# Row-tiled scores and a softplus split into a high and a low half, in the stick-breaking attention of a two-layer hybrid decoder step

## The reference, cut to what matters

```python
z = jnp.einsum('bqhd,bkhd->bhqk', qb, kb).astype(jnp.float32) * scale + bf
log_stop = jnp.where(mask, jax.nn.log_sigmoid(-z), 0.0)
after = lax.cumsum(log_stop, axis=3, reverse=True) - log_stop
A = jnp.where(mask, jnp.exp(jax.nn.log_sigmoid(z) + after), 0.0)
outs.append(jnp.einsum('bhqk,bkhd->bqhd', A.astype(v.dtype), vb))
```

## Time and profile before

| | |
|---|---|
| median of 3 runs | 1691.22 us (1683.71 to 1696.84) |
| span of the profiled execution | 1684.9 us |
| instructions in it | 22304 |
| mean granted TensorE clock | 0.956 |
| sweeps of the second layer, pair 0, 1, 2 | about 912 to 1055, 1135 to 1282, 1346 to 1525 us |

### The profile page before, as it was taken

The page is one execution under the profiler, slowest core; times in us unless marked ns, Lnnn a source line. Parts: engine busy times, 40 slices in busy tenths (PEclk is TensorE's granted clock), DMA queues, the critical chain, the costliest instruction groups (busy, mean ns, idle before and its releaser), DMA issues. The chain is left out here.

```text
span 1684.9 us, 22304 instructions
## 1 busy us (share of the span) xinstructions
PE 1550.3 (92%) x8356; PEld 1254.9 (74%) x8356; DVE 751.6 (45%) x1181; ACT 691.0 (41%) x1339; POOL 578.9 (34%) x471
## 2 busy tenths in 40 slices
PE   5899998999999999999759999989989999989995
PEld 3877698766797666899548767977658976669994
DVE  4332317976353334341661323278763533333417
ACT  5344512444524545443343344224444245445423
POOL 2353412535223333142443433115441242431325
PEclk8999979999999999999879999899999999999998
DMA  6400023100221000241252000230002200003213
GB/s 237 155 26 26 13 60 82 51 26 1 73 75 51 26 13 14 67 139 51 96 170 90 25 26 13 90 84 32 13 13 85 70 32 26 14 27 113 92 42 125
DMA packets 75672, 103.69 MB, mean 62 GB/s; under 512 B 14370, under 2 KB 61218, under 8 KB 75426
## 3 DMA queue, kind: packets, MB, share of 16 engines
q1 hardware_dynamic: 64176, 60.64, 11.1%
q10 hardware_dynamic: 11378, 41.53, 7.7%
HBM read 74.26 MB, written 27.88 MB: 61 GB/s over the span
## 5 line engine op out<-in xcount | busy, mean ns | idle before, releaser
L690 PE MATMUL ring<-H_hi,w_hi 128*128 128x352 f32 x1824 | 623.5, 342 | 19.7 <-DVE sb_q L1198 7.3
L692 PE MATMUL ring<-H_hi,w_lo 128*128 128x352 f32 x1824 | 597.0, 327 | 0.0
L691 PE MATMUL ring<-H_lo,w_hi 128*128 128x352 f32 x1824 | 596.9, 327 | 0.0
L690 PEld LDWEIGHTS ring<-H_hi,w_hi 128*128 128x128 f32 x1824 | 352.4, 193 | 72.1 <-issue 39.7
L691 PEld LDWEIGHTS ring<-H_lo,w_hi 128*128 128x128 f32 x1824 | 353.4, 194 | 5.9 <-issue 3.5
L692 PEld LDWEIGHTS ring<-H_hi,w_lo 128*128 128x128 f32 x1824 | 351.9, 193 | 0.0
L1415 POOL TENSOR_TENSOR w_lo<-w_raw,w_hi 128x1024 fp32r<-128x1024 f32 x76 | 188.7, 2484 | 372.0 <-ACT w_hi L893 372.0
L1479 POOL TENSOR_SCALAR attend<-attend 128x512 f32<-128x512 f32 (+4 forms) x144 | 177.3, 1248 | 273.8 <-ACT attend L959 273.5
L1165 DVE SCALAR_TENSOR_TENSOR attend<-Z,vec_sb,attend 128x512 f32<-128x512 f32 (+4 forms) x144 | 82.5, 612 | 217.1 <-ACT attend L967 217.0
L1274 DVE SCALAR_TENSOR_TENSOR MX<-MX,vec_sb 128x1023 f32<-128x1023 f32 (+29 forms) x120 | 158.2, 1318 | 0.3
L800 PE MATMUL Z<-sb_q,sb_k 128*128 128x512 f32 (+5 forms) x288 | 110.7, 498 | 0.0
(11 more groups left out here) (148 smaller groups left out, 1852.1 us busy)
## 6 DMA issues: line engine op xcount, KB each, us to landing
w_raw<-in_w ACTq DMA_DIRECT2D x76, 512.0 KB, 3.4
out_yT<-MX SPq DMA_DIRECT2D x6, 1408.0 KB, 9.3
attend<-out_yT SPq DMA_DIRECT2D x6, 1408.0 KB, 10.1
out_yT<-MX SPq DMA_DIRECT2D x12, 704.0 KB, 3.3
attend<-in_cache_k SPq DMA_DIRECT2D x96, 64.0 KB, 1.9
attend<-in_cache_v SPq DMA_DIRECT2D x96, 64.0 KB, 2.0
MX<-in_xT SPq DMA_DIRECT2D x3, 1408.0 KB, 11.8
out_k_rows<-sb_k SPq DMA_DIRECT2D x6, 528.0 KB, 2.8
```

The lines of the kernel that those rows point to most:

```text
L690: nc.tensor.matmul(in_ring(step), a, x, start=(k == 0), stop=False)
L691: nc.tensor.matmul(in_ring(step), a, y, start=False, stop=False)
L692: last = nc.tensor.matmul(in_ring(step), b, x, start=False, stop=(k == KB - 1))
```

## The change

**Scores.** `sb_q` holds each query once. Head h multiplies rows 64h to 64h+63 of the keys with the same rows of the queries, so each matmul uses 64 rows of the array, and the two write different banks. Both heads' score matmuls come first, then both masks. The samples' queries, which still need the zeroed form, have a small tile of their own (`own_q9`).

**High and low half.** After VectorE's maximum, ScalarE copies the softplus into `stop_hi` (rounded to `float32r`) and VectorE subtracts that from it into `stop_lo`. The triangle is multiplied with each, and so are the totals, in `float32r`. The totals no longer go to 64 partitions a head: a stationary tile of ones, zeros, ones (`side_r`), cut at 0 or at 64, puts head 0's total on partitions 0 to 63 and head 1's on 64 to 127, and all four matmuls add up in one bank. `stop` has two buffers instead of four; the exponential of unit u+1 waits for the low half of unit u, the copy for the triangle and total of unit u-1.

**Space.** For the new tiles, the rotation's buffer `rot_a` is gone: GpSimd writes its product into `ret_q` or `ret_k`, and VectorE adds to it there.

The core of the diff:

```diff
+        tri_r = sb("tri_r", [P, P], F32R)
+        side_r = sb("side_r", [P, 3 * HEAD_DIM], F32R)
+        stop_hi = sb("stop_hi", [P, 2, 512], F32R)
+        stop_lo = sb("stop_lo", [P, 2, 512], F32R)
...
-        sb_q = sb("sb_q", [P, 2, NT])
+        sb_q = sb("sb_q", [P, NT])
+        own_q9 = sb("own_q9", [P, 2, NS])
...
-        stop = part(4, 512)
+        stop = part(2, 512)
...
                     kb, q0, n = UNITS[u]
+                    if u >= 2:
+                        pe.wait_ge(s_a.sem, s_a.at((p, u - 2, 1)))
+                    elif u == 0:
+                        if p > 0:
+                            pe.wait_ge(s_a.sem, s_a.at((p - 1, "sample")))
+                        pe.wait_ge(s_q.sem, s_q.at(job_of("sq", p, CH - 1)))
+                        if p == 0:
+                            pe.wait_ge(s_masks, 16)
+                        pe.wait_ge(s_copy.sem, s_copy.at(job_of("sk", p, CH - 1)))
+                    diagonal = q0 == kb * P
                     for h in range(2):
-                        if u >= 2:
-                            pe.wait_ge(s_a.sem, s_a.at((p, u - 2, h)))
-                        elif h == 0 and u == 0:
-                            if p > 0:
-                                pe.wait_ge(s_a.sem, s_a.at((p - 1, "sample")))
-                            pe.wait_ge(s_q.sem, s_q.at(job_of("sq", p, CH - 1)))
-                            if p == 0:
-                                pe.wait_ge(s_masks, 16)
-                            pe.wait_ge(s_copy.sem, s_copy.at(job_of("sk", p, CH - 1)))
-                        bk = Z[2 * (u % 2) + h]
-                        diagonal = q0 == kb * P
-                        last = nc.tensor.matmul(bk[:, 0:n], sb_k[:, kb * P:(kb + 1) * P], sb_q[:, h, q0:q0 + n],
+                        r = slice(64 * h, 64 * h + 64)
+                        last = nc.tensor.matmul(Z[2 * (u % 2) + h][:, 0:n], sb_k[r, kb * P:(kb + 1) * P], sb_q[r, q0:q0 + n],
                                                 start=True, stop=not diagonal, skip_group_check=True)
-                        if diagonal:
-                            last = nc.tensor.matmul(bk[:, 0:P], ident_b[:], masks[:, 0:P], start=False, stop=True,
-                                                    skip_group_check=True)
-                        last.then_inc(s_z.sem, s_z.mark((p, u, h)))
+                        if not diagonal:
+                            last.then_inc(s_z.sem, s_z.mark((p, u, h)))
+                    if diagonal:
+                        for h in range(2):
+                            nc.tensor.matmul(Z[2 * (u % 2) + h][:, 0:P], ident_b[:], masks[:, 0:P], start=False, stop=True,
+                                             skip_group_check=True).then_inc(s_z.sem, s_z.mark((p, u, h)))
                 elif kind == "stop":
                     p, u = step[1:]
                     kb, q0, n = UNITS[u]
                     for h in range(2):
-                        pe.wait_ge(s_sp.sem, s_sp.at((p, u, h)))
-                        nc.tensor.matmul(Z[2 * (u % 2) + h][:, 0:n], negtri, stop[:, (2 * u + h) % 4, 0:n], start=False,
-                                         stop=True, skip_group_check=True).then_inc(s_za.sem, s_za.mark((p, u, h)))
+                        bk = Z[2 * (u % 2) + h][:, 0:n]
+                        pe.wait_ge(s_shi.sem, s_shi.at((p, u, h)))
+                        nc.tensor.matmul(bk, tri_r[:], stop_hi[:, h, 0:n], start=False, stop=False, skip_group_check=True)
+                        pe.wait_ge(s_slo.sem, s_slo.at((p, u, h)))
+                        nc.tensor.matmul(bk, tri_r[:], stop_lo[:, h, 0:n], start=False, stop=True,
+                                         skip_group_check=True).then_inc(s_za.sem, s_za.mark((p, u, h)))
                     if kb > 0:
                         if UNITS[u - 1][0] > 0:
                             pe.wait_ge(s_keepf.sem, s_keepf.at((p, u - 1)))
                         elif p > 0:
                             pe.wait_ge(s_keepf.sem, s_keepf.at((p - 1, U - 1)))
                         for h in range(2):
-                            last = nc.tensor.matmul(TOT[64 * h:64 * h + 64, 0:n], ones[:, 0:64], stop[:, (2 * u + h) % 4, 0:n],
-                                                    start=True, stop=True, skip_group_check=True)
+                            mine = side_r[:, 64 * h:64 * h + P]
+                            nc.tensor.matmul(TOT[:, 0:n], mine, stop_hi[:, h, 0:n], start=(h == 0), stop=False, skip_group_check=True)
+                            last = nc.tensor.matmul(TOT[:, 0:n], mine, stop_lo[:, h, 0:n], start=False, stop=(h == 1),
+                                                    skip_group_check=True)
                         last.then_inc(s_tot.sem, s_tot.mark((p, u)))
...
             def exp_scores(p, u):
                 kb, q0, n = UNITS[u]
-                if u >= 2:
-                    act.wait_ge(s_za.sem, s_za.at((p, u - 2, 1)))
-                    if UNITS[u - 2][0] > 0:
-                        act.wait_ge(s_tot.sem, s_tot.at((p, u - 2)))
-                elif p > 0:
-                    act.wait_ge(s_tot.sem, s_tot.at((p - 1, U - 1)))
                 for h in range(2):
+                    if u > 0:
+                        act.wait_ge(s_slo.sem, s_slo.at((p, u - 1, h)))
+                    elif p > 0:
+                        act.wait_ge(s_slo.sem, s_slo.at((p - 1, U - 1, h)))
                     act.wait_ge(s_z.sem, s_z.at((p, u, h)))
-                    nc.scalar.activation(stop[:, (2 * u + h) % 4, 0:n], Z[2 * (u % 2) + h][:, 0:n], ACT.Exp,
+                    nc.scalar.activation(stop[:, h, 0:n], Z[2 * (u % 2) + h][:, 0:n], ACT.Exp,
                                          bias=vv(V_BIAS + 2 * p + h)).then_inc(s_e.sem, s_e.mark((p, u, h)))
...
             def ln_scores(p, u):
                 n = UNITS[u][2]
                 for h in range(2):
-                    s = stop[:, (2 * u + h) % 4, 0:n]
+                    s = stop[:, h, 0:n]
                     act.wait_ge(s_min.sem, s_min.at((p, u, h)))
                     nc.scalar.activation(s, s, ACT.Ln, bias=1.0).then_inc(s_l.sem, s_l.mark((p, u, h)))
+            def high_scores(p, u):
+                n = UNITS[u][2]
+                for h in range(2):
+                    if u >= 1:
+                        act.wait_ge(s_za.sem, s_za.at((p, u - 1, h)))
+                        if UNITS[u - 1][0] > 0:
+                            act.wait_ge(s_tot.sem, s_tot.at((p, u - 1)))
+                    elif p > 0:
+                        act.wait_ge(s_tot.sem, s_tot.at((p - 1, U - 1)))
+                    act.wait_ge(s_sp.sem, s_sp.at((p, u, h)))
+                    nc.scalar.activation(stop_hi[:, h, 0:n], stop[:, h, 0:n], ACT.Copy).then_inc(
+                        s_shi.sem, s_shi.mark((p, u, h)))
...
                     if u == 0:
                         ln_scores(p, u)
+                        high_scores(p, u)
...
                     if u + 1 < U:
                         ln_scores(p, u + 1)
+                        high_scores(p, u + 1)
...
             def softplus(p, u):
                 n = UNITS[u][2]
                 for h in range(2):
-                    s = stop[:, (2 * u + h) % 4, 0:n]
+                    s = stop[:, h, 0:n]
                     dve.wait_ge(s_l.sem, s_l.at((p, u, h)))
                     nc.vector.scalar_tensor_tensor(out=s, in0=Z[2 * (u % 2) + h][:, 0:n], scalar=vv(V_BIAS + 2 * p + h), in1=s,
                                                    op0=ALU.add, op1=ALU.max).then_inc(s_sp.sem, s_sp.mark((p, u, h)))
+                for h in range(2):
+                    s = stop[:, h, 0:n]
+                    dve.wait_ge(s_shi.sem, s_shi.at((p, u, h)))
+                    nc.vector.tensor_tensor(stop_lo[:, h, 0:n], s, stop_hi[:, h, 0:n].bitcast(F32), ALU.subtract).then_inc(
+                        s_slo.sem, s_slo.mark((p, u, h)))
...
-                        for h in range(2):
-                            r = slice(64 * h, 64 * h + 64)
-                            last = nc.vector.tensor_scalar(sb_q[r, h, cs(c)], src[r], HEAD_DIM ** -0.5, None, ALU.mult)
+                        last = nc.vector.tensor_scalar(sb_q[:, cs(c)], src, HEAD_DIM ** -0.5, None, ALU.mult)
+                        if c == CH - 1:
+                            for h in range(2):
+                                r = slice(64 * h, 64 * h + 64)
+                                last = nc.vector.tensor_scalar(own_q9[r, h, :], src[r, CW - NS:CW], HEAD_DIM ** -0.5, None, ALU.mult)
...
+                    to = (ret_q if name == "rq" else ret_k)[:, cs(c)]
+                    nc.vector.tensor_tensor(to, to, raw_rot[:, n % 2, :], ALU.add).then_inc(s_rope.sem, s_rope.mark(step))
...
+                        to = (ret_q if name == "rq" else ret_k)[:, cs(c)]
+                        nc.gpsimd.tensor_tensor(to, raw_rot[:, n % 2, :], turn[:, 0, cs(c)], ALU.mult).then_inc(
                             s_rota.sem, s_rota.mark(use))
```

31 lines of the change are left out of this document (17 added, 14 removed).

## The result

The changed kernel takes 1676.9 us, median of 12 runs (1671.0 to 1681.5), beside 1690.2 for the kernel before, also of 12 (1674.9 to 1704.0): ratio 0.9943, 95% interval 0.9919 to 0.9968. It is faster by 0.6%: 10 us by the ratio, 13 by the medians. The forecast was 53 us less, 1638, with a range of 1605 to 1675. The profiled execution has a span of 1675.0 us, 9.9 less than before.

A forecast was written before the change was run, and what follows sets the result against it. TensorE, busy 92% of the span, was taken as the bound: 80.5 us saved there plus 2 for queries, less waits of 8, 15 and 6, gives 53.5 us, median 1638 us; range 1605 to 1675.

The forecast's parts named there:

- TensorE's work, 80.5 us saved: TensorE in the attention sweeps: scores save 21.3 us, triangle 42.1 and totals 17.1, together 80.5 us.
- rival 1: In the scores, row tiles run one after the other, giving -14.4 rather than 21.3 us; 1673 us; chance 0.12.
- Durations of copies and subtractions: Added per unit: two ScalarE copies of 0.516 us (74 us in all), two VectorE subtractions of 0.65 us (94 us).
- (a): Before the triangle: copy and subtraction after the softplus make TensorE wait in units 0 and 11; 8 us, between 4 and 16.
- (c): Retention evictions behind the copies on ScalarE, in 20 of 72 units, exposed in one of five: 6 us, between 0 and 30.
- (b): ScalarE's copy waits for VectorE's softplus, delaying work TensorE needs, chiefly in sweep 1: 15 us, between 5 and 35.
- Rival 2: VectorE's work holds sweeps 1 and 2, so (a) to (c) double: 1667 us, 1660 to 1685; chance 0.10.
- Rival 3: Copies and subtractions fully exposed in 48 units of sweeps 1 and 2, 112 us: slower, 1720 us; chance 0.06.
- within 1%: Case that the whole kernel's time stays within 1% of no change; chance 0.11.

The follow-up runs named there:

- short limit: GpSimd's limit on the exponential cut to 8 columns: in the changed kernel 1649.4 us (0.9796), in the kernel before 1687.3 us (1.0021).
- Short taps: The 28 convolution taps in pair 1's sweep cut to 8 columns: in the changed kernel 1654.4 us (0.9829), in the kernel before 1674.9 us (0.9939).
- the filling: Two extra fp32 matmuls ahead of each of nine retention steps in pair 1's sweep: changed kernel 1676.7 us (0.9953), kernel before 1698.8 us (1.0099).
- row tiles alone: The kernel before with only the row-tiled scores and one-step query eviction, triangle and totals still fp32 pairs: 1671.5 us (0.9916).

## Why the prediction was wrong, step by step

- *TensorE's work, 80.5 us saved*: right. The records give 85.0, row tiles run side by side (rival 1 is out), and one-pass matmuls cost what was put down.
- *Durations of copies and subtractions*: right for the copies, 0.59 for 0.65 us for the subtractions.
- *(a) The longer step before the triangle, 8 us*: too high. TensorE's matmuls waited 4.0 us for the high half and 1.2 for the low half in the whole kernel.
- *(c) Retention evictions behind the copies, 6 us (0 to 30)*: its mechanism is there, and its size was low. In the second sweep of pair 0 TensorE waited 3.8 us for `kd_tok`, where it was 0.8:

```profile
PE ring L704 <- ACT kd_tok L1103: 3.8, 3, 2.4
PE ring L704 <- DVE raw_rot L1290: 2.0, 1, 2.0
```

  If (a) and (c) are laid on the sweeps of pairs 0 and 2 alone, they were to take 14 us of 57 there (the forecast had part of both in pair 1; the sum is the same). The four sweeps gained 24, so 33 were taken: 21 as waits at full clock and 12 in stretches of the lower one. That is 19 us more than forecast.
- *(b) Sweep 1, "there the new work adds 1 to 2 us each and TensorE's saving isn't realized. 15 us for both layers, between 5 and 35"*: **this is the step that failed**. The sweeps of pair 1 were to give 2 x 14.7 less 15, some 14 us; they took 19 us. The term is short by 33 us. With the 19 of the line above that is 52; some 8 come back from the 4.5 more of work saved and from the stretches between the sweeps, and 44 are what the span missed (53.5 forecast, 9.9 measured). I looked only for the link from VectorE to ScalarE. I didn't follow what TensorE's saving runs into: the wait L715 for `kd` was in the trace of before with 1.7 us, behind a GpSimd limit of 2.6, and it grew to 3.1 when triangle and totals ahead of it became shorter. The pair of kernels with the short limit prices GpSimd's limit at 25 to 28 us of the 44, but only 15 of them in the sweeps of pair 1, where the change lost 48 (29 saved and not had, 19 longer). Short taps gave 22 us back in these two sweeps and would have given 10 without the change; the filling gave 4. No single one gives back half of the 48, and they weren't cut together, so what holds the rest of that sweep stays open. Rival 2 (1660 to 1685) named the sweep and blamed VectorE, and the 1677 us lie in its range. For the whole kernel VectorE's taps are the smaller part (the change is worth 19 us with them short, not sharply measured, and 38 with the limit short); in the sweeps of pair 1 the two parts are about alike (12 and 15 us), and they aren't independent, since GpSimd's operations are slower beside the taps.
- *The clock* had no term. 66 us more at the lower level are real. In the sweeps of pair 1 the filling bounds their cost between 4 and 17 us, in those of pairs 0 and 2, with 27 us of the 66, half of that is the most, 14. So a term of 4 to 31 us was put at nothing, and part of what the other terms are short by can be this one: the records can't tell a matmul that is late by the clock from one that would have waited. Of the 53 us, the 15 that the short limit still leaves stay open.
- *Rival 3*, slower: no. It takes 2.3 us in each of 48 units as 112 us; that product is 110, which changes nothing. *The chances*: "within 1%" had 0.11, and that is what came.

## What to carry to other kernels

Before pricing work removed from the busiest engine, go through every wait that this engine already has behind it, also the short ones, and follow each to the chain of the other engines that ends it: if that chain doesn't start with the removed work, the saving turns into wait, as 1.7 us did into 3.1. A busy share of 92% to 94% doesn't say how much can be taken out; adding work that waits for nothing helps to see it (23 us at no cost after the change, 15 us lost before it), but where the clock was low it also brings the clock back, and the two effects mix. The two layers of one kernel, or its own repeated executions, show what the clock alone costs, if they differ in nothing else. And a cut is best tested in both kernels: the short limit gave 25 us in one and none in the other, which no profile of one kernel alone would have told.

## What the runs showed of the hardware

- Two fp32 matmuls on different 64-row halves of the array, each into its own bank, run side by side: starts 0.006 us apart, 0.85 us for the pair at 384 columns and 1.06 at 512, against 1.29 and 1.72 over the whole array.
- The granted clock went to its lower level behind single TensorE pauses of 2.4 to 3.4 us in a sweep that was otherwise busy; behind the one at 1194.3 the windows read 0.54 and 0.61 for the next 8 us. It didn't do so behind each: a pause of 2.59 us stands at the same place of the changed kernel's sweep of pair 1 in both layers, and the clock fell behind it in the first and not in the second.
- With row tiles alone, 17 us more at 1.2 GHz made one of two otherwise equal sweeps 7.6 us longer.
- GpSimd's time for one and the same operation isn't constant: the decay L1468 on 128x256 took 1.28 us in the piece shown, where VectorE worked on taps without a pause, against a median of 729 ns over its 54 instructions. In the changed kernel the seven that took over 1.2 us all ran while taps did.
